# Decoder layer step: the second row block's statistics move behind the first weights' second halves, its transposes to the first tile's last eighth

## The chip, the cores and the metric

The kernel runs on one NeuronCore of a Trainium2 chip. The metric is the device time in microseconds (us) of one execution; lower is better. Comparisons use the median of several runs.

## The reference, cut to what matters

The reference computes one inference step of a hybrid decoder layer for two request groups: 512 new prompt rows and 8 x 8 = 64 sample rows, 1024 features each. The change touches only the very first part: the normalization of the rows and the first columns of the input projection.

```
def rmsnorm(x, g):
    xf = x.astype(jnp.float32)
    y = xf * lax.rsqrt(jnp.mean(xf * xf, axis=-1, keepdims=True) + NORM_EPS) * g.astype(jnp.float32)
    return y.astype(x.dtype)
...
    h = rmsnorm(x, norm1_g)
    xa, ga, q, k, v, gate_a, gate_b = jnp.split(jnp.einsum('btd,de->bte', h, w_in), IN_SPLITS, axis=-1)
```

Behind it come a recurrent branch, an attention branch with caches, their merge, and a feed-forward network, all fed with the same weights for both groups.

## The kernel before

**Precision by splitting.** Every fp32 product is made of three products of rounded parts. Each weight block w_raw (128 x 1024 values of one column block of 128, named a unit) is converted by ScalarE into its high part (w_s, part 0; hi_split, or hi_half for half a unit) and by VectorE into the rest (w_s, part 1; lo_split, lo_half). The normalized rows are split in the same way into h_hi and h_lo (x_hi on ScalarE, x_lo on VectorE).

**Row blocks.** The 576 rows form five blocks: four of 128 prompt rows (every fourth row) and one of 64 sample rows. Block r goes through a fixed chain:
- x_stat(r), ScalarE: the square with the row sum (L1057, followed by a read of the accumulator) and the root (L1059).
- x_scale(r), VectorE: the reciprocal (L1450) and the scaling of x_tok by it and by the gain (L1455), which raises x_norm.
- x_to_features(r), TensorE, the step named "Xr": eight transposes into PSUM (L674), which raise xT_ps. It waits for x_norm.
- x_hi(r), ScalarE: the rounding into h_hi (L1071 for r = 1 to 3).
- x_lo(r), VectorE: the rest into h_lo (L1469 for r = 1 to 3), which raises h_lo_rdy.

**Row tiles.** row_tile(hp, s) multiplies one row block by three units at once (384 columns). It runs over eight k-blocks of 128 features; a tile of prompt rows makes three matmuls for each (L639), 24 in all. Tile s = 0 is block 0, s = 1 is block 1, and so on to s = 4, all by the first three units. Tile s waits at its start until block s has been split (h_lo_rdy). Between its k-blocks it runs other steps: the dictionary X_AT says ahead of which k-block of tile s the transposes X(s+1) stand. In tile 0 there is a further wait ahead of k = 4, since the first three units come in halves: the first halves (k = 0 to 3) and the second halves (k = 4 to 7) have each a transfer, a conversion on ScalarE (hi_half(u, q), L1052) and one on VectorE (lo_half(u, q), L1445) of their own:

```
                for k in range(KT):
                    for step in between.get(k, "").split():
                        attend(hp, step)
                    if k in weights:
                        pe.wait_ge(lo_ready, weights[k])
                        pe.wait_ge(h_lo_rdy, 1 + k // 4)
```

**What sets the order.** Each engine works through its instructions in the order of the program text, and semaphores join the engines. SyncE's queue issues the loads: row block 0, the constants, three first halves, row block 1, three second halves, row blocks 2 to 4, then the next units. ScalarE's order at the start is x_stat(0), three first halves, x_hi(0), x_stat(1), three second halves, x_hi(1), x_stat(2). VectorE's is x_scale(0), three first halves, x_lo(0), x_scale(1), three second halves, gain_rows (two copies, L1479 and L1480), x_lo(1), x_scale(2). From there both go tile by tile.

Of the kernel before, what the change touches and what calls it, by code (L numbers as in the profile page):

```python
# [101 lines left out]
def ffn_steps():  # L102
    for i in range(NPAIR):
        yield "up", i, 0
        for r in range(NRND):
# [7 lines left out]
OWN_PE = {7: {1: "K0 K1 K2"}, 10: {3: "T0 T1"}, 11: {3: "T2 T3"}, 12: {1: "Q0 Q1 Q2"}, 13: {3: "T4 T5"}, 14: {0: "A0", 4: "T6 T7"}}  # L113
NEXT_PE = {0: {1: "B0"}, 1: {0: "P0", 4: "V0 S1"}, 2: {1: "P1 O0", 4: "V1 S2"}, 3: {1: "P2 O1", 4: "V2 S3"},
           4: {1: "P3 O2", 4: "V3 S4"}, 5: {1: "P4 O3", 4: "V4"}, 6: {1: "O4"}}
X_AT = {0: 4, 1: 4, 2: 2, 3: 2}


def build(nc, t):
# [39 lines left out]
    with ctx:  # L159
# [224 lines left out]
        def group(b, w):  # L384
            return b.rearrange("p (g d) -> p g d", d=w)

        def gbank(tl):
            return ps[0][:, 512 * (tl % 2):512 * (tl % 2) + GW]
# [220 lines left out]
        def _(pe):  # L609
# [226 lines left out]
            for hp in range(NH):  # L836
                for s in range(NSLOT):
                    steps = dict(OWN_PE.get(s, {}))
                    if hp:
                        steps.update(NEXT_PE.get(s, {}))  # L840
                    elif s in X_AT:
                        steps[X_AT[s]] = f"X{s + 1}"
                    elif s == 6:
# [187 lines left out]
        def _(act):  # L1031
# [17 lines left out]
            def hi_half(u, q):  # L1049
                act.wait_ge((raw_in, raw_half)[q][u], 16)  # L1050
                k = slice(4 * q, 4 * q + 4)
                A(w_s[:, u, 0, k, :], w_raw[:, u, k, :], ACT.Copy).then_inc(hi_ready, 1)  # L1052

            def x_stat(r):
                rows = NS if r == NCLS else P
                act.wait_ge(x_in[r], 16)
                A(x_sq[0:rows, :], x_tok[0:rows, r, :], ACT.Square, accum_out=xst[0:rows, 0, r:r + 1]).then_inc(x_sqd, 1)  # L1057
                act.wait_ge(x_sqd, r + 1)
                A(xst[0:rows, 1, r:r + 1], xst[0:rows, 0, r:r + 1], ACT.Sqrt, scale=1.0 / D, bias=eps[0:rows, :]).then_inc(x_root, 1)  # L1059

            def x_hi(r):
                bank = TRN if r % 2 else TQ
                if r:
                    act.wait_ge(xT_ps, r + 2)
                if r == 0:
                    for q in range(2):
                        k = slice(4 * q, 4 * q + 4)
                        act.wait_ge(xT_ps, q + 1)
                        A(h_hi[:, k, CLS[0]:CLS[0] + P], group(bank[:, 512 * q:512 * q + 512], P), ACT.Copy).then_inc(h_hi_rdy, 1)
                elif r < NCLS:  # L1070
                    A(h_hi[:, :, CLS[r]:CLS[r] + P], group(bank[:, :], P), ACT.Copy).then_inc(h_hi_rdy, 1)  # L1071
                else:
                    x = group(bank[:, 0:KT * NS], NS)
                    for a in range(2):
                        A(h_hi[:, :, HALF * a + 2 * P:HALF * (a + 1)], x[:, :, NS // 2 * a:NS // 2 * (a + 1)], ACT.Copy)
                    A(hs[:, :, 0:NS], x, ACT.Copy).then_inc(h_hi_rdy, 1)
# [111 lines left out]
            for u in range(3):  # L1188
                hi_half(u, 0)
            x_hi(0)  # L1190
            x_stat(1)
            for u in range(3):
                hi_half(u, 1)
            x_hi(1)
            x_stat(2)

# [228 lines left out]
        def _(dve):  # L1425
# [16 lines left out]
            def lo_half(u, q):  # L1442
                dve.wait_ge(hi_ready, 3 * q + u + 1)
                k = slice(4 * q, 4 * q + 4)
                TT(w_s[:, u, 1, k, :], w_raw[:, u, k, :], w_s[:, u, 0, k, :], ALU.subtract).then_inc(lo_ready, 1)  # L1445

            def x_scale(r):
                rows = NS if r == NCLS else P
                dve.wait_ge(x_root, r + 1)
                dve.reciprocal(xst[0:rows, 2, r:r + 1], xst[0:rows, 1, r:r + 1]).then_inc(x_rinv, 1)  # L1450
                dve.wait_ge(x_rinv, r + 1)
                if r == 0:
                    dve.wait_ge(row_ps, 1)
                for c in (slice(0, D // 2), slice(D // 2, D)) if r == 0 else (slice(0, D),):
                    STT(x_tok[0:rows, r, c], x_tok[0:rows, r, c], xst[0:rows, 2, r:r + 1], SC[0:rows, c],  # L1455
                        ALU.mult, ALU.mult).then_inc(x_norm, 1)

            def x_lo(r):
                bank = TRN if r % 2 else TQ
                if r:  # L1460
                    dve.wait_ge(h_hi_rdy, r + 2)
                if r == 0:
                    for q in range(2):
                        dve.wait_ge(h_hi_rdy, q + 1)
                        k, c = slice(4 * q, 4 * q + 4), slice(CLS[0], CLS[0] + P)
                        TT(h_lo[:, k, c], group(bank[:, 512 * q:512 * q + 512], P), h_hi[:, k, c], ALU.subtract).then_inc(h_lo_rdy, 1)
                elif r < NCLS:
                    c = slice(CLS[r], CLS[r] + P)
                    TT(h_lo[:, :, c], group(bank[:, :], P), h_hi[:, :, c], ALU.subtract).then_inc(h_lo_rdy, 1)  # L1469
                else:  # L1470
                    x = group(bank[:, 0:KT * NS], NS)
                    for a in range(2):
                        c = slice(HALF * a + 2 * P, HALF * (a + 1))
                        TT(h_lo[:, :, c], x[:, :, NS // 2 * a:NS // 2 * (a + 1)], h_hi[:, :, c], ALU.subtract)
                    TT(hs[:, :, NS:2 * NS], x, hs[:, :, 0:NS], ALU.subtract).then_inc(h_lo_rdy, 1)

            def gain_rows():
                dve.wait_ge(row_ps, 2)
                dve.tensor_copy(gkb[:, :], gbank(1))  # L1479
                dve.tensor_copy(gq[:, :], ps[0][:, 512 + GW:512 + GW + NG]).then_inc(row_taken, 1)  # L1480
# [139 lines left out]
            for u in range(3):  # L1620
                lo_half(u, 0)
            x_lo(0)
            x_scale(1)
            for u in range(3):
                lo_half(u, 1)
            gain_rows()
            x_lo(1)
            x_scale(2)
# [331 lines left out]
```

## Time and profile before

| | |
|---|---|
| median of 3 runs | 1171.07 us (1170.72 to 1171.48) |
| profiled execution, its own time | 1170.31 us |
| its span, first to last instruction | 1168.5 us |
| TensorE matmul busy | 1162.4 us (99%) |
| TensorE weight load busy | 1131.6 us (97%) |
| VectorE busy | 654.1 us (56%) |
| ScalarE busy | 454.7 us (39%) |
| GpSimd busy | 167.5 us (14%) |

The span is 1.8 us shorter than the time of the same execution, for what lies ahead of the first and behind the last instruction. Busy shares are means over the whole span; the change lies in the first 25 us of it, so that those have to be read by themselves.

### The profile page before, as it was taken

Reading aid. Unit: us, or ns where it says so; the run is one execution under the profiler, and the core shown is the slowest. Engines: PE = TensorE matmul, PEld = TensorE weight load, DVE = VectorE, ACT = ScalarE, POOL = GpSimd, SP = SyncE. Lnnn points to the kernel's source line nnn. Section 1 sums busy time; section 2 is a strip of 40 time slices with the busy share of each in tenths; the row PEclk is TensorE's granted clock in tenths of the full one; section 3 lists DMA queues with packets and bytes.
Section 4 is the critical chain, followed back from the end, with each engine's and each line's share of the span. In section 5 each row is a group of like instructions: output and inputs, shape, how many; then the busy total and the mean of one; then the engine's idle time right before and its main releaser. Section 6 shows DMA issues by size and latency. Waiting matters only on the chain.

```text
span 1168.5 us, 21547 instructions
## 1 busy us (share of the span) xinstructions
PE 1162.4 (99%) x8961; PEld 1131.6 (97%) x8961; DVE 654.1 (56%) x1333; ACT 454.7 (39%) x718; POOL 167.5 (14%) x261
## 2 busy tenths in 40 slices
PE   9999999999999999999999999999999999999998
PEld 7999999999999999999999999999999999999998
DVE  6553544625522355756545559878347884378741
ACT  6444444434423367676543443222212222122221
POOL 2374153252330000000100120000000000000000
PEclk9999999999999999999999999999999999999999
DMA  8576255354431222222353223232222323232232
GB/s 242 147 212 170 79 143 148 97 155 120 130 93 55 73 83 73 80 73 59 128 136 90 73 73 90 72 90 80 88 84 79 89 72 95 72 90 74 88 101 58
DMA packets 183492, 118.50 MB, mean 101 GB/s; under 512 B 7114, under 2 KB 175694, under 8 KB 183418
## 3 DMA queue, kind: packets, MB, share of 16 engines
q1 hardware_dynamic: 172352, 89.47, 26.9%
q0 software_dynamic: 11056, 28.01, 8.6%
q8 instruction: 50, 0.82, 0.3%
q14 instruction: 24, 0.20, 0.1%
q10 hardware_dynamic: 10, 0.01, 0.0%
HBM read 107.43 MB, written 8.45 MB: 99 GB/s over the span
## 4 chain that ended last, share of the span: by engine, by line
PE 99%; DVE 1%; ACT 0%; issue 0%; ACTq 0%; DVEq 0%
PE ps L660 66%; PE ps L639 20%; PE ps L961 2%; PE ps L729 1%; PE ps L716 1%; PE ps L876 1%; PE ps L772 1%; PE ps L797 1%; PE ps L793 1%; PE ps L741 1%; PE ps L803 1%; PE ps L757 1%; PE ps L760 1%; PE ps L682 0%; DVE w_s L1445 0%; PE ps L761 0%
## 5 line engine op out<-in xcount | busy, mean ns | idle before, releaser
L660 PE MATMUL ps<-h,w_s 128*128 128x288 f32 x3840 | 517.5, 296 | 0.0
L660 PEld LDWEIGHTS ps<-h,w_s 128*128 128x128 f32 x3840 | 512.6, 189 | 3.9 <-issue 3.9
L1439 DVE TENSOR_TENSOR w_s<-w_raw,w_s 128x1024 fp32r<-128x1024 f32 (+1 forms) x160 | 193.9, 1212 | 221.2 <-ACT w_s L1047 221.1
L1047 ACT ACTIVATE w_s<-w_raw 128x1024 fp32r<-128x1024 f32 (+1 forms) x160 | 166.3, 1039 | 334.9 <-PE ps L660 330.3
L639 PE MATMUL ps<-w_s,h 128*128 128x384 f32 x1152 | 217.4, 341 | 0.9 <-DVE w_s L1445 0.5
L639 PEld LDWEIGHTS ps<-w_s,h 128*128 128x128 f32 x1152 | 198.6, 188 | 2.8 <-DVE w_s L1445 0.7
L660 PE MATMUL ps<-g_hi,w_s 128*128 128x288 f32 x672 | 119.1, 297 | 0.0
L660 PEld LDWEIGHTS ps<-g_hi,w_s 128*128 128x128 f32 x672 | 99.4, 189 | 0.0
L660 PE MATMUL ps<-g_lo,w_s 128*128 128x288 f32 x336 | 71.9, 296 | 0.0
L601 POOL DMA_DIRECT2D out<-f_row x6 | 3.4, 567 | 415.1 <-ACT f_row L1393 415.1
L660 PEld LDWEIGHTS ps<-g_lo,w_s 128*128 128x128 f32 x336 | 54.1, 189 | 0.0
L1387 ACT ACTIVATE g_hi<-gm 128x576 fp32r<-128x576 f32 x24 | 16.5, 685 | 92.9 <-DVE gm L1872 92.9
L660 PE MATMUL ps<-mg_hi,w_s 128*128 128x288 f32 x256 | 46.5, 298 | 0.0
L660 PE MATMUL ps<-y_hi,w_s 128*128 128x288 f32 x256 | 44.9, 296 | 0.0
L1525 DVE TENSOR_REDUCE nrm<-sq 128x3 f32<-128x384 f32 (+1 forms) x40 | 22.0, 549 | 40.6 <-ACT sq L1104 35.1
L1151 ACT ACTIVATE prob<-prob,stat 128x512 f32<-128x512 f32 (+1 forms) x20 | 15.1, 756 | 70.6 <-DVE stat L1597 70.6
L639 PE MATMUL ps<-w_s,hs 128*128 128x384 f32 x192 | 38.4, 342 | 0.0
L660 PEld LDWEIGHTS ps<-mg_hi,w_s 128*128 128x128 f32 x256 | 38.0, 189 | 0.0
L660 PEld LDWEIGHTS ps<-y_hi,w_s 128*128 128x128 f32 x256 | 37.8, 189 | 0.0
L1592 DVE CUSTOM_DVE_ANT_0 prob<-ps,masks 128x256 f32<-128x256 f32 (+2 forms) x40 | 16.2, 442 | 34.5 <-PE ps L761 29.8
L639 PEld LDWEIGHTS ps<-w_s,hs 128*128 128x128 f32 x192 | 33.0, 188 | 0.8 <-issue 0.8
L1104 ACT ACTIVATE sq<-ps 128x384 f32<-128x384 f32 x32 | 15.8, 492 | 45.6 <-PE ps L639 45.6
(303 smaller groups left out, 1427.7 us busy)
## 6 DMA issues: line engine op xcount, KB each, us to landing
w_raw<-in_w_in SPq DMA_DIRECT2D x65, 512.0 KB, 3.9
w_raw<-in_w_up SPq DMA_DIRECT2D x48, 512.0 KB, 3.9
w_raw<-in_w_down SPq DMA_DIRECT2D x24, 512.0 KB, 3.8
kc<-in_cache_k_g POOLq DMA_DIRECT2D x48, 128.0 KB, 3.2
vc<-in_cache_v_g POOLq DMA_DIRECT2D x12, 512.0 KB, 6.4
w_raw<-in_w_out SPq DMA_DIRECT2D x8, 512.0 KB, 3.8
w_raw<-in_w_br_a SPq DMA_DIRECT2D x7, 512.0 KB, 3.9
x_tok<-in_x_prompt SPq DMA_DIRECT2D x4, 512.0 KB, 8.4
```

Of the source, the lines that this page charges most:

```text
L639: last = mm(group(gbank(tl), HD), x, w_s[:, w0:w0 + 3, part, k, :], start=(k == 0 and n == 0), stop=(k == KT - 1 and n == len(terms(k)) - 1))
L660: last = mm(pu[u % 2][:, 512 * a:512 * a + HALF], w[:, part, k, :], x[:, k, HALF * a:HALF * (a + 1)], start=(k == 0 and i == 0), stop=(k = ...
L716: tr(feature_bank(g)[:, r * P:(r + 1) * P], buf[:, r, g, :], ident)
L729: last = tr(key_bank(b)[:, i * P:(i + 1) * P], kc[:, n % NKC, i, :], ident)
L961: last = mm(pu[u % 2][:, 512 * a:512 * a + HALF], w_s[:, ring(u), part, k, :], x[:, k, HALF * a:HALF * (a + 1)], start=(start and i == 0), ...
L1047: A(w_s[:, ring(u), 0, 0:nkt[u], :], w_raw[:, u % NRAW, 0:nkt[u], :], ACT.Copy).then_inc(hi_ready, 1)
L1104: A(sq[:, :], gbank(tl), ACT.Square).then_inc(sq_rdy, 1)
L1151: A(pr, pr, ACT.Exp, bias=stat[:, e % 4, 2:3], accum_out=stat[:, e % 4, 3:4]).then_inc(p_ready, 1)
L1387: A(g_hi[r % 2][:, i % PPR, :], gm[:, :], ACT.Copy).then_inc(g_hi_rdy, 1)
L1439: TT(w_s[:, ring(u), 1, 0:nkt[u], :], w_raw[:, u % NRAW, 0:nkt[u], :], w_s[:, ring(u), 0, 0:nkt[u], :], ALU.subtract).then_inc(lo_ready, 1)
L1525: dve.tensor_reduce(nrm[0:rows, 0, NG * r:NG * (r + 1)], group(sq[0:rows, :], HD), AX_X, ALU.add).then_inc(ss_done, 1)
L1592: last = dve.tensor_tensor_reduce(prob[:, s0:s0 + n], SC[:, s0:s0 + n], masks[:, m - C_PM:m - C_PM + n], SCALE, -3e38, ALU.add, ALU.max, s ...
```

## The change

On ScalarE x_stat(1) moves from ahead of the three second halves to behind them; on VectorE x_scale(1) does the same. On TensorE the transposes X1 of row block 1 move, within tile 0, from ahead of k = 4 (and ahead of the wait for the second halves) to ahead of k = 7. No instruction is added or removed, and the loads keep their order.

```
-X_AT = {0: 4, 1: 4, 2: 2, 3: 2}
+X_AT = {0: 7, 1: 4, 2: 2, 3: 2}
...
             for u in range(3):
                 hi_half(u, 0)
             x_hi(0)
-            x_stat(1)
             for u in range(3):
                 hi_half(u, 1)
+            x_stat(1)
             x_hi(1)
             x_stat(2)
...
             for u in range(3):
                 lo_half(u, 0)
             x_lo(0)
-            x_scale(1)
             for u in range(3):
                 lo_half(u, 1)
+            x_scale(1)
             gain_rows()
             x_lo(1)
             x_scale(2)
```

## Rows read from the trace of the kernel before

**Rows 1.** The page: span, TensorE's busy time, its granted clock in 40 slices.

```profile
span 1168.5 us, 21547 instructions
...
PE 1162.4 (99%) x8961; PEld 1131.6 (97%) x8961; DVE 654.1 (56%) x1333; ACT 454.7 (39%) x718; POOL 167.5 (14%) x261
...
PEclk9999999999999999999999999999999999999999
```

**Rows 2.** Everything that TensorE's matmuls waited for, whole span: us, times, longest.

```profile
PE ps L682 <- DVE sq L1617: 1.3, 1, 1.3
PE ps L948 <- DVE x L1898: 0.6, 1, 0.6
PE ps L639 <- DVE w_s L1445: 0.5, 1, 0.5
PE ps L639 <- DVE h L1469: 0.4, 1, 0.4
```

**Rows 3.** The chain that ended last, 12.5 to 25 us: start us, us, what.

```profile
12.53 1.28 DVE x_tok L1455
13.81 1.82 DVE w_s L1445 x3
...
15.67 4.43 PE ps L639 x24
20.10 0.89 PE ps L674 x8
...
21.01 1.03 ACT h L1071
...
22.07 1.24 DVE h L1469
23.31 0.14 issue
23.44 1.30 PE ps L639 x6
```

**Rows 4.** Timeline of TensorE, 11.9 to 15.2 us: start, duration, engine, line, operation.

```profile
11.96 2.32 PE L639 MATMUL ps<-w_s,h 128*128 128x384 f32 x12
14.12 1.03 PE L674 MATMUL ps<-const,x_tok 128*128 128x128 f32 x8
```

**Rows 5.** Timeline of ScalarE, 10.8 to 19.2 us.

```profile
10.81 1.06 ACT L1057 ACTIVATE x_sq<-x_tok 128x1024 f32<-128x1024 f32 x1
11.76 0.21 ACT L1057 ACTIVATION_READ_ACCUMULATOR x_sq<-x_tok 128x1 f32 x1
12.00 0.29 ACT L1059 ACTIVATE xst<-xst,const 128x1 f32<-128x1 f32 x1
12.20 1.40 ACT L1052 ACTIVATE w_s<-w_raw 128x512 fp32r<-128x512 f32 x2
13.83 0.63 ACT L1052 ACTIVATE w_s<-w_raw 128x512 fp32r<-128x512 f32 x1 [0.23 <-DMA w_raw<-in_w_in]
15.19 1.03 ACT L1071 ACTIVATE h<-ps 128x1024 fp32r<-128x1024 f32 x1 [0.73 <-PE ps L674]
...
18.14 1.06 ACT L1057 ACTIVATE x_sq<-x_tok 128x1024 f32<-128x1024 f32 x1 [0.55 <-DMA x_tok<-in_x_prompt]
```

**Rows 6.** Timeline of VectorE, 11.1 to 17.5 us.

```profile
11.13 1.28 DVE L1466 TENSOR_TENSOR h<-ps,h 128x512 fp32r<-128x512 f32 x2
12.33 0.16 DVE L1450 RECIPROCAL xst<-xst 128x1 f32<-128x1 f32 x1
...
15.53 0.55 DVE L1479 COPY gkb<-ps 128x384 f32<-128x384 f32 x1
...
16.25 1.22 DVE L1469 TENSOR_TENSOR h<-ps,h 128x1024 fp32r<-128x1024 f32 x1
```

**Rows 7.** Loads of the second halves: issue starts; the last's time to landing.

```profile
L442 SPq DMA_DIRECT2D w_raw<-in_w_in x3: 463/745/1054, 3.8 to 5.4; - x3
...
w_raw<-in_w_in SPq DMA_DIRECT2D x1, 256.0 KB, 8.4
```

More of the change, by code:

```diff
@@ L115 @@
            4: {1: "P3 O2", 4: "V3 S4"}, 5: {1: "P4 O3", 4: "V4"}, 6: {1: "O4"}}
-X_AT = {0: 4, 1: 4, 2: 2, 3: 2}
+X_AT = {0: 7, 1: 4, 2: 2, 3: 2}
 def build(nc, t):
@@ L1190, in _ @@
             x_hi(0)
-            x_stat(1)
             for u in range(3):
                 hi_half(u, 1)
+            x_stat(1)
             x_hi(1)
@@ L1622, in _ @@
             x_lo(0)
-            x_scale(1)
             for u in range(3):
                 lo_half(u, 1)
+            x_scale(1)
             gain_rows()
```

## The prediction

> **What bounds the kernel now.** I read the page first: TensorE's matmuls are busy for 1162.4 of 1168.5 us, and its clock is granted in full in all 40 slices [rows 1]. The reader is to see that there is hardly any idle time from which a change could take something. The waits of TensorE over the whole span come next: beside 1.3 us at the very start there are three, of 0.6, 0.5 and 0.4 us [rows 2]. The first is at the very end (the last sum), the other two lie in the stretch of this change. No wait later on ends with a transfer or with anything that runs by a clock of its own. So a delay of TensorE in the first 25 us is not taken back later: what follows is TensorE's own work, and it moves to the end in full. The chain of waits, third, shows the two places at the start: VectorE's rest of the second halves releases TensorE at 15.67 us, and the rest of row block 2 releases it at 23.44 us [rows 3]. The timelines of the single engines, last, give the price of each link.
>
> **TensorE in this stretch.** The 24 matmuls from 15.67 us (12 of tile 0, 12 of tile 1) take 4.43 us, 0.1846 us each [rows 3]. Tile 0's first 12 start at 11.96 us and so end their issue at 14.17; the eight transposes X1 begin at 14.12 and end at 15.15 us, almost entirely inside the wait for the second halves [rows 4]. Tile 0's last 12 then run until 15.67 + 12 x 0.1846 = 17.88 us, when tile 1 starts. Row block 1 was ready for it: its rest ended at 16.25 + 1.22 = 17.47 us [rows 6], and with the 0.14 us that lie between the rest of block 2 and the matmul behind it [rows 3] tile 1 could have begun at 17.61. The chain of block 1 has 0.27 us of slack, no more.
>
> **What moves on ScalarE.** Nothing is added or removed; the price is in the order. Before, x_stat(1) begins at 10.81 us and its root ends at 12.29; the third conversion of the second halves then begins at 13.83, after 0.23 us of waiting for its data [rows 5]. Those data left SyncE's queue at 5.4 us and took 8.4, so they land at 13.8 us [rows 7]. The loads keep their order, so they land there again. So x_stat(1) filled time in which ScalarE had nothing else that it could finish with. After the change it stands behind the third conversion: 13.83 + 0.63 = 14.46, less the 0.11 us by which a next instruction's record begins ahead of the end of the one before it (11.76 against 10.81 + 1.06), about 14.35 us [rows 5]. The square of block 1 is 14.35 - 10.81 = 3.54 us later. The conversions win almost nothing: the first may start before 12.20, but the third, which decides, still waits for 13.83.
>
> ScalarE's order could only be passed over if a later instruction went ahead of a waiting one. ScalarE stood idle for 0.23 us ahead of 13.83 us [rows 5]. The Trainium skill (TensorE: Matmul & The Clock Gate, section "Architectural detail: the array is 16× 32×32, not 1× 128×128") says that ScalarE and VectorE work strictly first in, first out. That rule speaks against this change: by it the square cannot use the wait, and the sum is the one below; if the queue could let it pass, the square would keep its place and the sum would be near nothing. Those rows are in keeping with the rule, but in them nothing ready stood behind the wait, so they do not prove it.
>
> **What moves on VectorE.** Before, the reciprocal and the scaling of block 1 (12.33 to 13.81 us) stand ahead of the three rests of the second halves, 1.82 us for three, which end at 15.63 [rows 3, 6]. After it, the first two rests are done as their high parts come (those are ready by 13.60, the end of the two conversions in rows 5; so by 13.60 + 0.61 = 14.21), and the third starts when the third conversion ends, 14.46; it takes a third of 1.82, 0.61 us, and standing alone a tenth more, which the records of neighbours overlap: 15.15 us. TensorE's k = 4 then starts at about 15.2 instead of 15.67 us. That is the gain, 0.45 us. It can't be more, since the data land at 13.8. It is used up at once: X1, which before took 0.87 us in the shadow of that wait, now stands between tile 0's matmuls, in the open. Were nothing else late, tile 1 would begin at 15.2 + 12 x 0.1846 + 0.89 (transposes as X2 in rows 3) = 18.3 us, 0.4 later than now.
>
> **The chain of block 1 after the change.** From the start of its square (10.81) to the end of its rest and tile 1 (17.61) it is now 6.80 us without a stop: square and root, scaling until 13.81 [rows 3, 5], 0.31 to the first transpose, 1.03 of transposes [rows 4], 1.03 of rounding from 15.19 [rows 5], the rest until 17.47 [rows 6], and 0.14. Each engine is free for its link: VectorE ends the third rest at 15.15 and gain_rows, which now stands between the scaling's end at 17.35 and the rest's start at about 19.8, is a copy of 0.55 us [rows 6] and one of three columns, and fits in there. So it starts at 14.35 and lets tile 1 begin at 21.15 us. In the chart of TensorE: 9 matmuls from 15.2 to 16.9; the scaling ends at 17.35, X1 runs from 17.66 to 18.7; 3 matmuls until about 19.1; then 2 us of waiting for the rest of block 1. Tile 1 starts at 21.15 instead of 17.88 us: **+3.3 us**.
>
> **What is late next.** Behind x_hi(1) ScalarE has x_stat(2), VectorE x_scale(2) behind x_lo(1). The rounding of block 1 ends at 15.19 + 1.03 + 3.54 = 19.76 us; block 2's square would start at about 19.7 and its scaling end at about 22.5 us (19.7 + 3.0 of a chain like block 1's, with VectorE's link 0.1 later than ScalarE's); X2 comes when TensorE has done 12 matmuls of tile 1, 21.15 + 2.22 = 23.4. It is in time. Block 3 lies 1.5 us behind it (18.14 waited only for its transfer, which is in by then [rows 5]) and is in time too. From X2 on the pattern is that of before: X2, rounding, rest, tile 2, with the 0.38 us of waiting at 23.44 [rows 3] kept, all 3.3 us later. SyncE's loads of the next units wait for the rests of the first three, which come some tenths earlier; GpSimd's caches wait for TensorE, which is not idle for them. Nothing takes the 3.3 us back.
>
> **Sum.** On the profiled execution's own time, 1170.31 + 3.3 = 1173.6 us; the median of the runs lies 0.76 above it, so 1171.07 + 3.3 = 1174.4 us, +0.28%. I take 1174.3, since X1's slot may save a tenth. Faster or slower by 0.2% is 2.3 us, about what a measurement of this kernel can tell from no change. Own range of this case: 1173.4 to 1175.3 (a DMA landing within some tenths, twice).
>
> **Rivals.**
>
> *The data come earlier than in the profile.* The profiled execution is one; if the second halves landed before ScalarE asks for them (at 10.8, where x_stat(1) now begins), x_stat(1) would be behind three conversions and no wait: 1.40 + 0.63 less an overlap, 1.9 us later [rows 5]. That gives 17.61 + 1.9 = 19.5 us for tile 1, +1.6 us, 1172.7 us. For it: nothing but that loads vary. Against it: the last landing is 13.8 us by the profile, and the next transfers were also waited for (0.55 us at 18.14 [rows 5]).
>
> *The clock falls.* TensorE idles 1.0 us at 14.2, 0.7 at 16.9 and 2.0 at 19.1, more than half of the 7 us between 14.2 and 21.15. Before, its longest wait is 1.3 us [rows 2], and the clock is full throughout [rows 1], so no row shows what 2 us do. If the lower of its two levels (1.2 instead of 2.4 GHz) were granted for the first 12 matmuls of tile 1, they would take up to 2.2 us more; for 24, up to 4.4. Sum: +3.3 + 2.2 = +5.5, 1176.6 us, at most 1178.8. The Trainium skill (TensorE: Matmul & The Clock Gate, section "Part 1: The HAM clock gate (the "warmup" mystery)") says that the engine rests at the lower level and that activity releases it; no row here shows the lower level.
>
> *Not slower.* TensorE restarts 0.45 us earlier for the second halves, and block 1's chain is not late. This needs the square of block 1 to begin no later than 11.1 to 11.5 us, that is, the second halves' third conversion to be through more than 2 us before its data land. Price then: from -0.25 to +0.4 us, 1170.8 to 1171.5. More than 0.9 us, the sum of the two waits there, could not be won in any case. It would also be so if the later chain absorbed the delay; rows 2 show no wait that could.
>
> **Chances.** The forecast 0.68; data earlier 0.12; the clock 0.13; not slower 0.05, of which 0.02 I leave for a real gain by something that I do not see; 0.02 for other slower ones. Slower by over 0.2%: 0.68 + 0.13 + 0.02 = 0.83. Within 0.2%: 0.12 + 0.03 = 0.15. Faster: 0.02. The range goes from the early data (1172.7; I take 1172.8) to the lower clock for 12 matmuls (1176.6), which leaves out half of the first rival, the upper half of the second and the third, about 0.17.
>
> **What would show it.** Right: the square of block 1 (L1057) begins at about 14.4 us, right behind the third conversion at about 13.8; matmuls resume at about 15.2; X1 at about 17.7 with 0.7 us of waiting for the scaling ahead of it; a wait of about 2 us for L1469 ahead of tile 1 at about 21.2; tile 2 at 26.7 instead of 23.44; span 1171.8; the waits of TensorE longer by 3 us in sum. Wrong: second halves landing early, tile 1 before 20 us, a slice with a clock under 9, or a shift at 25 us that has grown smaller at the end of the span.

## The result: 0.27% slower, and the profile after

The changed kernel takes 1174.29 us (median of 17 runs, 1172.21 to 1176.33), the kernel before 1170.67 us (17 runs beside them, 1169.93 to 1172.26). The medians are 3.6 us apart; the ratio, which is not taken from the two medians alone and so lies a little under their quotient of 1.0031, is 1.0027 (3.2 us), 95% interval 1.0021 to 1.0034. The profiled execution of the changed kernel took 1176.02 us, so it is one of the long ones of the 17, and it shows more than the median does. One of the 27 executions of the kernel before that stand beside e1 to e4 took 1295.64 us at a mean clock of 0.818; it is left out of every comparison.

Its page, span, busy times and granted clock in 40 slices:

```profile
span 1174.2 us, 21547 instructions
...
PE 1164.4 (99%) x8961; PEld 1132.6 (96%) x8961; DVE 654.5 (56%) x1333; ACT 454.6 (39%) x718; POOL 167.5 (14%) x261
...
PEclk9999999999999999999999999999999999999999
```

Against [rows 1] the span is 5.7 us longer, TensorE's busy time only 2.0 us. The rest is waiting, and these are its waits over the whole span:

```profile
PE ps L639 <- DVE h L1469: 2.3, 2, 1.9
PE ps L639 <- DVE w_s L1445: 1.5, 1, 1.5
PE ps L682 <- DVE sq L1617: 1.3, 1, 1.3
PE ps L948 <- DVE x L1898: 0.6, 1, 0.6
PE ps L639 <- DVE h L1466: 0.5, 1, 0.5
PE ps L674 <- DVE x_tok L1455: 0.3, 1, 0.3
```

Against [rows 2] the wait for L1469 (the rest of a row block) has grown from 0.4 to 2.3 us, that for L1445 (the rest of the second halves) from 0.5 to 1.5 instead of shrinking; the last two are new. ScalarE's timeline tells why the second halves are late as well:

```profile
12.37 0.63 ACT L1052 ACTIVATE w_s<-w_raw 128x512 fp32r<-128x512 f32 x1 [0.44 <-DMA w_raw<-in_w_in]
13.70 0.63 ACT L1052 ACTIVATE w_s<-w_raw 128x512 fp32r<-128x512 f32 x1 [0.69 <-DMA w_raw<-in_w_in]
14.82 0.63 ACT L1052 ACTIVATE w_s<-w_raw 128x512 fp32r<-128x512 f32 x1 [0.50 <-DMA w_raw<-in_w_in]
15.36 1.04 ACT L1057 ACTIVATE x_sq<-x_tok 128x1024 f32<-128x1024 f32 x1
...
19.52 1.02 ACT L1071 ACTIVATE h<-ps 128x1024 fp32r<-128x1024 f32 x1 [2.70 <-PE ps L674]
```

The last half landed at 14.8 us, not at the 13.8 of [rows 5], with the same loads in the same order ahead of it. ScalarE now waits three times for data, 1.6 us in all, with row block 1 standing behind it; before, the square of block 1 lay in that time. It begins at 15.36 instead of 10.81 us. TensorE's timeline (the last row is cut off by the window that was read):

```profile
12.43 2.32 PE L639 MATMUL ps<-w_s,h 128*128 128x384 f32 x12 [0.47 <-DVE h L1466]
16.23 1.85 PE L639 MATMUL ps<-w_s,h 128*128 128x384 f32 x9 [1.47 <-DVE w_s L1445]
18.39 1.09 PE L674 MATMUL ps<-const,x_tok 128*128 128x128 f32 x8 [0.31 <-DVE x_tok L1455]
19.24 0.77 PE L639 MATMUL ps<-w_s,h 128*128 128x384 f32 x3
21.95 3.88 PE L639 MATMUL ps<-w_s,h 128*128 128x384 f32 x12 [1.94 <-DVE h L1469]
25.67 1.04 PE L674 MATMUL ps<-const,x_tok 128*128 128x128 f32 x8
26.46 2.33 PE L639 MATMUL ps<-w_s,h 128*128 128x384 f32 x12
29.17 1.12 PE L639 MATMUL ps<-w_s,h 128*128 128x384 f32 x5 [0.38 <-DVE h L1469]
```

Tile 1 begins at 21.95 instead of 17.88 us, +4.07. Its first 12 matmuls then take 3.88 us where the 12 behind X2 take 2.33. Tile 2 begins at 29.17 instead of 23.44, +5.73, of which 5.73 - 4.07 = 1.66 us arose within tile 1; at the end of the span the shift is still 5.7. The clock stands in the rows by stretch (the third number from the end, behind the busy times of the five engines):

```profile
20.00:22.00 2.00, 0.06 (x2) 0.08 (x1) 1.28 (x2) 1.97 (x5) 0.00 (x0) 1.00 0.81 211
22.00:24.00 2.00, 2.00 (x7) 2.00 (x8) 1.93 (x4) 1.24 (x3) 0.00 (x0) 0.53 1.03 236
24.00:26.00 2.00, 2.00 (x11) 1.96 (x10) 0.81 (x1) 0.00 (x0) 0.00 (x0) 0.62 0.69 250
26.00:28.00 2.00, 2.00 (x16) 2.00 (x15) 0.20 (x1) 1.26 (x2) 0.00 (x0) 1.00 0.08 31
```

TensorE did next to nothing from 20 to 22 us, and then, from just after 22 us until about 25.5, the lower level, 1.2 GHz, was granted (0.53 and 0.62 of full speed as means of two stretches that have a little of the full level at either end). The 12 matmuls of tile 1 ahead of X2 took 25.67 - 21.95 = 3.72 us from the first start to X2's; e8 below has the same 12 at the full clock in 2.16. So 4.1 of the 5.7 us are order and landing, about 1.6 are clock.

The page's slices could not show it. Each is 1174.2 / 40 = 29 us long, and 3.4 us at half speed leave its mean at 0.94, which is still a 9. The 9s of [rows 1] say the same little: the clock in a stretch of some microseconds has to be read from that stretch.

### The profile page after: what moved, and what is told of

It reads as the page before. It is cut to its first block, busy times and chain, and to the rows that moved or that the text cites. A ratio compares the mean times of both kernels' runs of the same rounds, so it can differ in the third digit from the quotient of the medians.

```text
span 1174.2 us, 21547 instructions
## 1 busy us (share of the span) xinstructions
PE 1164.4 (99%) x8961; PEld 1132.6 (96%) x8961; DVE 654.5 (56%) x1333; ACT 454.6 (39%) x718; POOL 167.5 (14%) x261
## 4 chain that ended last, share of the span: by engine, by line
PE 98%; DMA 1%; SPq 0%; ACT 0%; DVE 0%; issue 0%; ACTq 0%
PE ps L660 66%; PE ps L639 20%; PE ps L961 2%; PE ps L729 1%; PE ps L716 1%; PE ps L876 1%; PE ps L772 1%; PE ps L797 1%; DMA w_raw<-in_w_in 1%; PE ps L793 1%; PE ps L741 1%; PE ps L803 1%; PE ps L757 1%; PE ps L760 1%; PE ps L761 0%; PE ps L674 0%
## 5 line engine op out<-in xcount | busy, mean ns | idle before, releaser
L639 PE MATMUL ps<-w_s,h 128*128 128x384 f32 x1152 | 219.5, 342 | 4.3 <-DVE h L1469 2.3
L639 PEld LDWEIGHTS ps<-w_s,h 128*128 128x128 f32 x1152 | 200.0, 189 | 6.6 <-issue 2.8
L639 PE MATMUL ps<-w_s,hs 128*128 128x384 f32 x192 | 38.4, 342 | 0.0
L639 PEld LDWEIGHTS ps<-w_s,hs 128*128 128x128 f32 x192 | 33.0, 188 | 0.8 <-issue 0.8
```

Source lines behind the costliest of these rows:

```text
L639: last = mm(group(gbank(tl), HD), x, w_s[:, w0:w0 + 3, part, k, :], start=(k == 0 and n == 0), stop=(k == KT - 1 and n == len(terms(k)) - 1))
```

## The experiments

At the start one theory stood against several rivals. **A:** row block 1's chain (square, scaling, transposes, rounding, rest) has next to no slack, so any late link moves tile 1; the lower clock comes on top in some executions. **The rivals:** only one of the two edits costs (B: in e1 the order of the engines, in e2 X1's place), the chain is late by ScalarE's square alone (C), the clock plays no part in the median (D). Later ones are that the landing of the weights is the whole cause (E), that X1's move has a fixed price (F), and G for a small edit of its own in e5.

Only the profiled executions show when the clock fell; the others have its mean over the span alone. The three profiles with the lower level in the first 30 us (the changed kernel, e1, e2) have a mean of 0.998, the seven without it 0.999 or 1.000; 0.999 is seen there because the clock also falls behind the last matmul, while the last stores drain (in e3 0.81 of full speed is granted from 1168 to 1170 us, and TensorE does nothing there). So 0.998 or less is taken below as a sign of the lower level. It is not a sure one: 2 of the 27 executions of the kernel before that stand beside e5 to e8 have 0.998 too.

**e1: only X1's place.**

```
 (kernel before)
-X_AT = {0: 4, 1: 4, 2: 2, 3: 2}
+X_AT = {0: 7, 1: 4, 2: 2, 3: 2}
```

> The kernel before with one edit: X1 stands ahead of k = 7 of tile 0 instead of k = 4; ScalarE's and VectorE's orders stay. Theory A (row block 1's chain has only 0.27 us of slack, and whatever delays any link of it delays tile 1): k = 4 resumes at 15.67 us as before, X1 comes behind 9 matmuls at 17.3, its rounding ends at 19.4, the rest at 20.7, tile 1 starts at about 20.8 instead of 17.88: +2.9 us, and up to 1.7 more where the lower clock is granted behind the 2 us of idling: 1173.6 to 1175.3 us. Rival B (it is the square of block 1 behind the second halves that costs, X1's place is free): within 1 us of the kernel before, since the scaling is done at 13.8.

Measured: 1174.57 us, ratio 1.0036 (1.0023 to 1.0050). TensorE's timeline:

```profile
15.26 1.86 PE L639 MATMUL ps<-w_s,h 128*128 128x384 f32 x9 [1.39 <-DVE w_s L1445]
16.96 1.03 PE L674 MATMUL ps<-const,x_tok 128*128 128x128 f32 x8
...
20.46 3.51 PE L639 MATMUL ps<-w_s,h 128*128 128x384 f32 x12 [1.94 <-DVE h L1469]
```

VectorE's scaling of block 1:

```profile
12.12 1.28 DVE L1455 SCALAR_TENSOR_TENSOR x_tok<-x_tok,xst,ps 128x1024 f32<-128x1024 f32 x1
```

Theory A's picture to a few tenths, and B falls: the scaling was done at 12.12 + 1.28 = 13.4 us here, the transposes came at 16.96 all the same, and tile 1 waits 1.94 us. One edit of the three costs as much as all of them, within the intervals. The lower clock is there too (12 matmuls in 3.51 us, and 0.50 of full speed granted from 22 to 24 us); 3 of 5 executions have a mean of 0.998 or less. One of these has 0.996 and took 1177.98 us; it has no profile. The two at 0.999 took 1173.59 and 1174.52 us.

**e2: only the order on ScalarE and VectorE.**

```
 (changed kernel)
-X_AT = {0: 7, 1: 4, 2: 2, 3: 2}
+X_AT = {0: 4, 1: 4, 2: 2, 3: 2}
```

> The changed kernel with X1 back ahead of k = 4; ScalarE's and VectorE's orders as changed. Theory A: TensorE stops at 14.2 us until the scaling of block 1 is done (17.4 in an execution whose second halves land at 13.8, a microsecond later where they land at 14.8), X1 until 18.7, 12 matmuls until 20.9, tile 1 at about 21.2: +3.3 us as in the full change; the two edits hide each other and do not add. The idling is one piece of about 3.5 us instead of three, so that the lower clock should come at least as often; 1174 to 1176 us. Rival B (X1's place is the cost, the order is free): within 1 us of before. If the two parts add up instead, the two together would be the 3.6 us measured and each about half of it.

Measured: 1173.30 us, ratio 1.0023 (1.0014 to 1.0032), a little under the range expected. TensorE's timeline:

```profile
11.74 2.32 PE L639 MATMUL ps<-w_s,h 128*128 128x384 f32 x12
18.15 1.97 PE L674 MATMUL ps<-const,x_tok 128*128 128x128 f32 x8 [4.09 <-DVE x_tok L1455]
19.77 5.22 PE L639 MATMUL ps<-w_s,h 128*128 128x384 f32 x24
```

X1 waits 4.09 us for the scaling. Alone this edit costs +2.2 us (1171.12 beside it), X1's place alone +3.5, both together +3.6: they do not add, because each makes the same chain late and tile 1 waits for its end alone. The clock is mixed into these three medians, but the executions without its sign say the same: +1.7 us here, +2.5 and +3.4 in e1's two, +2.4 for both together. The lower clock came in 5 of 11 executions; in the profile it was granted from X1 on (0.53 of full speed from 18 to 20 us), right behind the wait.

**e3: ScalarE's order back.**

```
 (changed kernel)
+            x_stat(1)
             for u in range(3):
                 hi_half(u, 1)
-            x_stat(1)
```

> The changed kernel with x_stat(1) back ahead of the second halves on ScalarE; x_scale(1) stays behind them on VectorE and X1 ahead of k = 7. Theory A: VectorE ends the third rest at 15.2 us and the scaling at 16.5, X1 waits for 9 matmuls until 16.9, tile 1 starts at about 20.3 instead of 17.88: +2.4 us (1173.1), with the lower clock up to 1.7 more. Rival C (ScalarE's square is the one late link): about +0.4 us, within a microsecond of the kernel before. The difference to the changed kernel, about 0.9 us, is what the square's place costs by itself.

Measured: 1173.25 us, ratio 1.0020 (1.0011 to 1.0029). TensorE's timeline:

```profile
14.95 1.84 PE L639 MATMUL ps<-w_s,h 128*128 128x384 f32 x9 [0.51 <-DVE w_s L1445]
16.63 1.04 PE L674 MATMUL ps<-const,x_tok 128*128 128x128 f32 x8
...
20.14 2.33 PE L639 MATMUL ps<-w_s,h 128*128 128x384 f32 x12 [1.94 <-DVE h L1469]
```

Tile 1 at 20.14, 0.2 from what A said, and the time is 2.1 us above the kernel before and not 0.4; C falls. The restart of k = 4 at 14.95 is the gain that the change aims at, and it is worth nothing here, since X1 then stands behind nine matmuls. The lower clock came in none of 11 executions.

**e4: matmuls in the wait.**

```
 (changed kernel, row_tile)
+                if tl == 1:
+                    for _ in range(10):
+                        mm(group(gbank(1), HD), h[:, 0, 0, 0:P], w_s[:, 0:3, 0, 0, :], start=True, stop=True)
                 if tl < NTL:
                     pe.wait_ge(h_lo_rdy, tl + 2 if tl else 1)
```

> The changed kernel with ten more matmuls of the same form (1.85 us) into the bank that tile 1 overwrites, ahead of tile 1's wait for block 1. They lie in a wait of about 2 us and their result is not used. Theory A with the clock: the profile shows the clock full at tile 1, its first 12 matmuls take 2.2 us instead of 3.9, and the time is 1 to 1.7 us below the changed kernel's 1174.3: 1172.6 to 1173.3, with less spread between executions. Rival D (the clock seen in the one profile plays no part in the median, the order accounts for all of the 3.6 us): same as the changed kernel, or up to 0.3 us slower where the ten last longer than the wait.

Measured: 1173.17 us, ratio 1.0017 (1.0007 to 1.0026), 1172.53 to 1174.22 in 11 executions; none has a mean clock under 0.999. TensorE's timeline (L642 is L639 here, L1448 is L1445 and L1472 is L1469; L626 are the ten):

```profile
15.48 1.85 PE L642 MATMUL ps<-w_s,h 128*128 128x384 f32 x9 [0.38 <-DVE w_s L1448]
...
19.09 1.90 PE L626 MATMUL ps<-w_s,h 128*128 128x384 f32 x10
21.11 2.38 PE L642 MATMUL ps<-w_s,h 128*128 128x384 f32 x12
...
26.83 1.30 PE L642 MATMUL ps<-w_s,h 128*128 128x384 f32 x6 [0.38 <-DVE h L1472]
```

The ten fill the wait and tile 1 runs at the full clock, 12 matmuls in 2.38 us. More work, and less time than the changed kernel by 1.1 us (1174.29 - 1173.17). The two intervals overlap, so that the medians alone would not decide it; the sign of the lower clock in none of 11 executions, against 10 of the changed kernel's 22, does. D falls. What is left, +2.05 us against 1171.12 beside it, is the order alone; its interval reaches from 0.8 to 3.0 us.

**e8: the changed kernel again**, unedited, on the chip of the next three.

> The changed kernel itself, unedited, on the chip of the runs below: 1174.3 us, ratio 1.0027 to the kernel before. It gives the measure for the loads' order beside it, and a second profile: with second halves that land at 13.8 to 14.1 us tile 2 should begin at about 27 us at the full clock and 28.5 us at the lower one.

Measured: 1175.62 us (1172.85 to 1175.69 in 5 executions), ratio 1.0036 (1.0022 to 1.0049). The median is 1.3 us above what was expected: three executions have a mean clock of 0.998 and took 1175.6 to 1175.7, the other two 1172.85 and 1173.04. The profiled one took 1172.85. TensorE's and ScalarE's timelines:

```profile
12.61 4.14 PE L639 MATMUL ps<-w_s,h 128*128 128x384 f32 x21
16.73 1.09 PE L674 MATMUL ps<-const,x_tok 128*128 128x128 f32 x8
...
20.29 2.33 PE L639 MATMUL ps<-w_s,h 128*128 128x384 f32 x12 [1.94 <-DVE h L1469]
22.45 1.04 PE L674 MATMUL ps<-const,x_tok 128*128 128x128 f32 x8
...
25.95 1.30 PE L639 MATMUL ps<-w_s,h 128*128 128x384 f32 x6 [0.37 <-DVE h L1469]
```

```profile
13.16 0.63 ACT L1052 ACTIVATE w_s<-w_raw 128x512 fp32r<-128x512 f32 x1 [0.23 <-DMA w_raw<-in_w_in]
13.70 1.05 ACT L1057 ACTIVATE x_sq<-x_tok 128x1024 f32<-128x1024 f32 x1
```

The last half landed at 13.1 us and tile 0 had begun 0.65 us later than before, so that TensorE ran through k = 4 without a stop, 21 matmuls in a row. And still tile 2 begins at 25.95, 2.51 us later than before; the span is 2.5 us longer. This is the change in its mildest form: early data, full clock, +2.5. It also settles rival E, ahead of the run that was made for it: the weights landed 0.7 us earlier than in the kernel before, and the time did not come back. The two profiles of one kernel are 3.2 us apart, 1.66 by the landing (21.95 against 20.29 for tile 1) and 1.56 by the clock.

**e6: row block 1's load behind the second halves.**

```
 (changed kernel, SyncE)
-            sp.dma_start(x_tok[:, 1, :], x_rows[1]).then_inc(x_in[1], 16)
             for u in range(3):
                 load_half(u, 1)
+            sp.dma_start(x_tok[:, 1, :], x_rows[1]).then_inc(x_in[1], 16)
```

> The changed kernel with row block 1's load issued behind the three second halves instead of ahead of them, so that the loads stand in the order in which ScalarE now takes them. Theory A (the square of block 1 is late because ScalarE must first wait for the second halves' landing): the halves land up to 1.7 us earlier (512 KB at about 300 GB/s), at 12.1 us or so, row block 1 at about 13.8, and the square begins there or up to 0.5 us earlier than now; tile 1 at about 20.6 to 21.0: 0.2 to 0.7 us better than the changed kernel, 1173.6 to 1174.1, still above the kernel before. Rival E (landing in general is the cause, any earlier weights give the time back): 2 us better than the changed kernel, about 1172.

Measured: 1172.93 us, ratio 1.0020 (1.0011 to 1.0029). ScalarE's timeline:

```profile
13.13 0.63 ACT L1052 ACTIVATE w_s<-w_raw 128x512 fp32r<-128x512 f32 x1 [0.81 <-DMA w_raw<-in_w_in]
14.39 1.06 ACT L1057 ACTIVATE x_sq<-x_tok 128x1024 f32<-128x1024 f32 x1 [0.63 <-DMA x_tok<-in_x_prompt]
```

TensorE ran its 21 matmuls without a stop, and then waited 1.0 us at X1 (from the waits of this kernel); tile 1 began at 21.00, as A said. The median is 0.7 to 1.2 us under what A expected and 0.9 above what E did, and the interval overlaps the changed kernel's, so the medians decide nothing between the two. Nor did the swap do in the profile what it was made for: the third conversion begins at 13.13 us, and in e8, with the old order, at 13.16, where 12.1 was expected. What the profile adds is small but on A's side: the weights were in, the square then waited for its own rows, and tile 1 came later than in e8 (21.00 against 20.29). 3 of the 11 executions have a mean clock of 0.998. Neither order of the loads brings the time of before back; against E stands e8.

**e7: X1 ahead of k = 5.**

```
 (kernel before)
-X_AT = {0: 4, 1: 4, 2: 2, 3: 2}
+X_AT = {0: 5, 1: 4, 2: 2, 3: 2}
```

> The kernel before with X1 ahead of k = 5 of tile 0 (e1 had k = 7, the kernel before has k = 4). Theory A (each k-block in front of X1 pushes tile 1 by its three matmuls, and one lost shadow comes on top): k = 4 resumes at 15.67 us, X1 from 16.2, its rest at about 19.6, tile 1 at about 19.7 instead of 17.88: +1.8 us, 1172.9, against +2.9 for k = 7; about 0.8 us of waiting ahead of tile 1 and no lower clock. Rival F (a fixed price for leaving the wait's shadow, whatever the place): the same +2.9 or more as with k = 7.

Measured: 1172.93 us, ratio 1.0019 (1.0010 to 1.0028), about half of what e1 cost. TensorE's timeline:

```profile
16.67 0.79 PE L639 MATMUL ps<-w_s,h 128*128 128x384 f32 x3 [1.36 <-DVE w_s L1445]
17.30 1.03 PE L674 MATMUL ps<-const,x_tok 128*128 128x128 f32 x8
18.09 1.82 PE L639 MATMUL ps<-w_s,h 128*128 128x384 f32 x9
20.80 2.33 PE L639 MATMUL ps<-w_s,h 128*128 128x384 f32 x12 [0.90 <-DVE h L1469]
```

In this profile everything is 1 us late from the start of tile 0 on (12.96 us). TensorE's first seven matmuls tell why, in the kernel before and here:

```profile
2.13 3.85 PE L682 MATMUL ps<-sq 128*128 128x384 f32 x7
```

```profile
2.12 4.69 PE L682 MATMUL ps<-sq 128*128 128x384 f32 x7
```

In the trace they start 0.64 us apart at first and 0.32 later. The step comes at about 5.0 us in the kernel before and at 7.1 here, and there the first record of the granted clock begins, at the full level. So this microsecond belongs to the execution and not to the edit: tile 1 begins 20.80 - 17.88 = 2.92 us later, 1.00 of it from the start.

What counts is the wait ahead of tile 1: 0.90 us here, 1.94 with k = 7; six matmuls at 0.185 us are 1.1 us. So the price grows with the place, and F falls, by the profile; the interval (1.2 to 3.3 us) would still hold the +2.9 of F. +1.9 us was measured (1170.99 beside it), +1.8 expected. No lower clock was expected; the profile has none, but 2 of the 11 executions have a mean of 0.998 (1173.62 and 1173.73 us).

**e5: X2 one k-block earlier.**

```
 (kernel before)
-X_AT = {0: 4, 1: 4, 2: 2, 3: 2}
+X_AT = {0: 4, 1: 3, 2: 2, 3: 2}
```

> The kernel before with the transposes of block 2 ahead of k = 3 of tile 1 instead of k = 4. The scaling of block 2 is done at 19.1 us and TensorE reaches k = 3 at 19.5, so X2 comes 0.55 us earlier and costs nothing more. Theory A: the wait of 0.38 us ahead of tile 2 (for L1469) is gone from the profile and tile 2 begins at 23.1; the time is 0.4 us below the kernel before, 1170.6 to 1170.8, which the runs can hardly tell from no change. Rival G (X2 then waits for the scaling): a wait at L674 of some tenths in place of it, time as before.

Measured: 1170.41 us against 1170.99 beside it, ratio 0.9996 (0.9987 to 1.0005): not to be told from no change. All of TensorE's waits:

```profile
PE ps L682 <- DVE sq L1617: 1.3, 1, 1.3
PE ps L660 <- DVE w_s L1435: 0.6, 1, 0.6
PE ps L948 <- DVE x L1898: 0.6, 1, 0.6
PE ps L639 <- DVE w_s L1445: 0.5, 1, 0.5
```

The wait for L1469 is gone, as A said. Rival G falls with it: no wait for the scaling (L674) has come in its place. In this execution another wait of 0.6 us stands at 589 us, for a weight load that took 10.0 us from issue to landing in the chain; whether it has to do with the edit stays open.

## Why the prediction was right, and where it was not

The time, the sign and the place were right: 1174.3 us forecast, 1174.29 measured. The sum behind it was right in its mechanism, but that it came out to a hundredth is luck: two errors cancel, an order priced too high and a clock that was left out.

**Right.** The square of block 1 stands right behind the third conversion: 15.36 behind 14.82, 13.70 behind 13.16. The wait ahead of tile 1 is the 2 us forecast, 1.94 in both profiles (and in e1, e3 and e6: it goes with X1's place alone). From the square to tile 1 it is 6.59 us in both (21.95 - 15.36, 20.29 - 13.70), forecast 6.80: the 0.31 us between the scaling and the first transpose were TensorE's own queue, and are some 0.05 where it stands idle. The wait of 0.38 us ahead of tile 2 is kept. Nothing takes the shift back: 5.73 us at tile 2 and 5.7 at the end, 2.51 and 2.5 in the second profile. In e4 it was 3.4 and 2.9: some 0.5 us came back between 565 and 600 us there, as in e7, for a reason that was not looked for. That the 0.45 us gained at k = 4 is worth nothing was shown by e3 and by e8, where there is no wait there at all and the kernel is still slower.

**Mis-sized: the landing and the step to the median.** The forecast took one landing, 13.8 us. In the changed kernel's profiles it was 14.8 and 13.1, in e2's and e4's 14.6 and 14.1 (the starts of the third conversion). The +3.3 us for the order are in the middle of the two profiles' +4.07 and +2.41 for tile 1, but against the median of before they are too many: e4, with the full clock, is +2.05 us. The profiled execution of before was quicker than the median of its runs, by 0.76 us with the three that were known ahead, by 0.36 with the 17 beside the result and by 0.81 with the 27 beside e4. I carried the 0.76 over to the median as if it were an offset. Without it the forecast would have been 1173.6, and e4 is 1173.17.

One place where it may lie is the clock at the very start, seen in e7. In the ten profiles the full level is first granted between 4.2 us (e1) and 7.1 us (e7), and tile 0 begins between 11.55 and 12.96 us in the same sequence, about 0.5 us later for each microsecond (in the changed kernel's first profile, 0.47 us of waiting for weights come on top). Where VectorE's order is that of before (e1, e5, e7), k = 4 of tile 0 shifts by the same amount; in e3, e4, e6 and e8 a late start is taken out of the wait for the second halves, which is shorter there or gone. So a late start would cost the kernel before and not the changed one, and the difference of the medians would be smaller than that to a profile of before with an early start (5.0 us, where the mean of the ten is 5.4). That this is where the 1 us went is argued from these numbers, not shown by a run of its own.

**Mis-sized: the clock, a rival at 0.13.** It is part of the result. Of the 17 executions 7 have a mean clock of 0.998, median 1174.65 us; the other 10 have a median of 1173.06 (two of these took 1174.8 and 1175.4; what made them long stays open, since no profile shows their landing). In e8 it was 3 of 5, and in e4, with TensorE kept busy, it is gone; it is also gone in e3, without any filling. Its price is 1.6 us in the profile (3.72 us for the 12 matmuls, 2.16 in e8), not the 2.2 allowed for them. The single starts in the trace show why: at the lower level the matmuls of tile 1 are 0.320 us apart, at the full one, in e8, 0.174, a factor of 1.84 and not of 2, and the lower level lasted for eleven of the 12. By the ratios, the 3.2 us measured (1.0027) are about 2.0 us of order (1.0017 in e4) and, at the median, about 1.2 us of clock, where the forecast had 3.3 us of order alone. The ten executions of the changed kernel without the sign, 2.4 us above the median of before, put the order a little higher. The prediction's sign of a wrong forecast, "a slice with a clock under 9", could not have shown this: 3.4 us at half speed do not bring a slice of 29 us under 9.

**The rivals.** "The data come earlier" came half way in e8's profile: the third half still kept ScalarE waiting for 0.23 us, the square stood at 13.70 and not at 12.7, and the price was +2.5 us instead of +1.6. "Not slower" is excluded by all executions of the changed kernel (none under 1172.21).

**A term that was put at next to nothing: X1's place.** The prediction gave the weight to the square's place on ScalarE. For X1 ahead of k = 7 with nothing else late it had tile 1 at 18.3 us, +0.4, and its rival "not slower" asked only that the square begin by 11.1 to 11.5 us. That counts the transposes themselves and leaves out the rounding and the rest, which follow them and which tile 1 needs. In e1 the square began at 10.41 us and the scaling ended at 13.4, and tile 1 began at 20.46, +2.58, with its wait of 1.94 us. The forecast of the whole change is not touched, since its chart has both parts; but with X1 ahead of k = 7 the chain would have been late by nearly as much had the square stayed where it was (e1, e3).

## What to carry to other kernels

A step that lies in the shadow of a wait is free only there: the eight transposes cost nothing while TensorE waited for weights, and moving them behind that wait cost both their own time and, through the two links behind them (rounding and rest), two microseconds of waiting ahead of the next tile. Before moving the start of a chain, compare its end with the time at which its consumer arrives; 0.27 us of slack do not bear a move of 3 us, and it makes no difference which link is the one that is late. And do not carry the difference between a profiled execution and the median over as an offset when it may lie in the very stretch that the change rewrites.

## What the runs showed of the hardware

The lower clock needed no stop longer than 2 us. In the changed kernel's first profile TensorE stood still for 1.47, 0.31 and 1.94 us with matmuls between them, and from just after 22 us the clock was at the lower level for 3.4 us. The stops do not settle it: in e1 (1.39 and 1.94 us) and e2 (one of 4.09) the profiles have the lower level, in e8 (1.94), e6 (0.99 and 1.94) and e3 (0.51 and 1.94) they do not. By the means of all executions it came in 10 of 22 of the changed kernel, 3 of 5 in e1, 5 of 11 in e2, 3 of 11 in e6, 2 of 11 in e7 and none of 11 in e3, e4 and e5. The Trainium skill (TensorE: Matmul & The Clock Gate, section "Part 1: The HAM clock gate (the "warmup" mystery)") says that the engine rests at the lower level and activity releases it; the two levels and the return under load agree with these rows. At the start of the program, under the same seven matmuls, the full level came at 4.2 to 7.1 us in ten profiles, and tile 0 up to 1.4 us later for it.

The matmuls of 384 columns with a weight load each start 0.320 us apart at the lower level and 0.174 at the full one (changed kernel's first profile and e8), a factor of 1.84; the seven with which the program opens go from 0.64 to 0.32, a factor of 2. The landing of a transfer with an unchanged queue ahead of it differed by 1.7 us between two executions of one kernel (14.8 and 13.1 us), about as much as the clock costs.
